# Attention beside projections: small matmuls of one step grouped by array shape, local probabilities turned two slots sooner

## The reference

```python
def stick_breaking_attention(q, k, v):      # 8 heads of 64
    for blk in range(S // BLOCK):           # blocks of 128 queries, keys 0 to the block's end
        z = jnp.einsum('bqhd,bshd->bhqs', qb, kb).astype(jnp.float32) * scale
        strict = s_idx < t_idx
        log_keep = jnp.where(strict, -jax.nn.softplus(z), 0.0)
        tail = lax.cumsum(log_keep, axis=3, reverse=True) - log_keep
        w = jnp.where(strict, jnp.exp(jax.nn.log_sigmoid(z) + tail), 0.0)
        outs.append(jnp.einsum('bhqs,bshd->bqhd', w.astype(v.dtype), vb))

def sliding_window_sink_attention(q, k, v, sinks):   # 8 query heads, 2 key heads, window 128
    scores = jnp.einsum('bnqkgd,bnskd->bnkgqs', qb, k_band).astype(jnp.float32) * scale
    scores = jnp.where(valid[None, :, None, None], scores, -jnp.inf)
    probs = jax.nn.softmax(jnp.concatenate([scores, sink], axis=-1), axis=-1)[..., :-1]
    out = jnp.einsum('bnkgqs,bnskd->bnqkgd', probs.astype(v.dtype), v_band)
```

## Time and profile before

| | |
|---|---|
| median of 3 runs | 2659.11 us (2658.48 to 2659.41) |
| the profiled execution | 2658.53 us |
| its span, first to last instruction | 2657.0 us |
| mean granted clock of TensorE | 0.999 |
| projections, L466 to L468 | 10248 matmuls recorded of 512 columns, 390 to 402 ns each, overlapping |
| first and second attention stage | about 1279 to 1465 us, 1981 to 2168 us |

### The profile page before, as it was taken

How to read it: one execution, slowest core, us unless ns; L and a number is a source line. 1 busy time by engine, 2 the same in 40 slices (tenths; PEclk the granted TensorE clock), 3 DMA queues, 4 the chain that set the end, 5 groups by cost and what they waited for, 6 DMA issues and landing times.

```text
span 2657.0 us, 32191 instructions
## 1 busy us (share of the span) xinstructions
PE 2625.0 (99%) x13046; PEld 2106.6 (79%) x13054; DVE 1514.9 (57%) x2100; ACT 1143.0 (43%) x1694; POOL 161.2 (6%) x147
## 2 busy tenths in 40 slices
PE   8999999999999999999999999999999999999998
PEld 6777778888887888888767888888877778888887
DVE  4566657474778665667765554433456754544433
ACT  6444344242467433335566334322346652423322
POOL 2222010000010000000111000000001100000000
PEclk9999999999999999999999999999999999999999
DMA  4111113222333323322211322223321123223332
GB/s 170 60 60 60 53 55 111 96 95 96 111 95 95 107 95 99 100 96 95 72 59 61 96 95 94 97 95 99 99 80 56 56 80 95 95 95 96 101 97 72
DMA packets 66674, 235.38 MB, mean 89 GB/s; under 512 B 7520, under 2 KB 8160, under 8 KB 66528
## 3 DMA queue, kind: packets, MB, share of 16 engines
q1 hardware_dynamic: 63504, 228.35, 26.7%
q10 hardware_dynamic: 3024, 4.99, 0.6%
HBM read 231.21 MB, written 2.10 MB: 88 GB/s over the span
## 4 chain that ended last, share of the span: by engine, by line
PE 89%; DVE 6%; ACT 3%; issue 2%; DMA 0%; POOL 0%; SPq 0%; ACTq 0%; DVEq 0%
PE bank L466 27%; PE bank L468 27%; PE bank L467 27%; DVE w_lo_k L1490 1%; PE bank L815 1%; PE bank L836 1%; ACT w_hi_k L985 1%; PE bank L885 1%; PE bank L825 1%; DVE xr_lru L1801 0%; PE bank L903 0%; PE bank L893 0%; DVE kept_att L1920 0%; PE bank L676 0%; DVE rot_att L1948 0%
## 5 line engine op out<-in xcount | busy, mean ns | idle before, releaser
L466 PE MATMUL bank<-x_hi_k,w_hi_k 128*128 128x512 f32 x2152 | 865.7, 402 | 12.1 <-DVE x_lo_k L1497 11.2
L468 PE MATMUL bank<-x_hi_k,w_lo_k 128*128 128x512 f32 x2152 | 840.6, 391 | 0.0
L985 ACT ACTIVATE w_hi_k<-raw_k 128x1024 fp32r<-128x1024 f32 x431 | 454.7, 1059 | 895.2 <-PE bank L468 893.6
L467 PE MATMUL bank<-x_lo_k,w_hi_k 128*128 128x512 f32 x2152 | 839.5, 390 | 0.0
L1490 DVE TENSOR_TENSOR w_lo_k<-raw_k,w_hi_k 128x1024 fp32r<-128x1024 f32 x431 | 534.7, 1241 | 166.2 <-ACT w_hi_k L985 165.7
L466 PEld LDWEIGHTS bank<-x_hi_k,w_hi_k 128*128 128x128 f32 x2152 | 404.7, 188 | 110.7 <-issue 14.6
L468 PEld LDWEIGHTS bank<-x_hi_k,w_lo_k 128*128 128x128 f32 x2152 | 404.6, 188 | 86.4
L467 PEld LDWEIGHTS bank<-x_lo_k,w_hi_k 128*128 128x128 f32 x2152 | 405.2, 188 | 82.1 <-issue 4.1
L466 PE MATMUL bank<-y_hi_k,w_hi_k 128*128 128x512 f32 x1136 | 445.6, 392 | 3.2 <-DVE y_lo_k L1836 1.9
L468 PE MATMUL bank<-y_hi_k,w_lo_k 128*128 128x512 f32 x1136 | 442.9, 390 | 0.0
L467 PE MATMUL bank<-y_lo_k,w_hi_k 128*128 128x512 f32 x1136 | 442.8, 390 | 0.0
(11 more groups left out here) (319 smaller groups left out, 2277.1 us busy)
## 6 DMA issues: line engine op xcount, KB each, us to landing
raw_k<-wstream SPq DMA_DIRECT2D x431, 512.0 KB, 3.5
outT<-h_k ACTq DMA_DIRECT2D x8, 256.0 KB, 2.8
h_k<-xT SPq DMA_DIRECT2D x4, 256.0 KB, 8.7
h_k<-xT ACTq DMA_DIRECT2D x4, 256.0 KB, 8.1
decay_mix<-constants ACTq DMA_DIRECT2D x4, 256.0 KB, 2.7
vec_k<-vectors SPq DMA_DIRECT2D x1, 282.5 KB, 10.3
cos_mix<-constants SPq DMA_DIRECT2D x1, 256.0 KB, 10.0
sin_mix<-constants SPq DMA_DIRECT2D x1, 256.0 KB, 10.2
```

The lines of the kernel that those rows point to most:

```text
L466: pe.matmul(dst, wh, rh, start=start, stop=False)
L467: pe.matmul(dst, wh, rl, start=False, stop=False)
L468: return pe.matmul(dst, wl, rh, start=False, stop=stop)
L985: act.activation(k.w_hi[:, u % SPLIT, :], k.raw[:, u % RAW, :], ACT.Copy).then_inc(*hi_done.mark())
```

## The change

TensorE's two lists become one, `pairs_in_step`. All of a step's logits, local scores, outputs and local outputs now stand together in slot 4 of the step, in this order: local masks, logit masks, logits, local scores, output of the step before, local output. So masks are written first (`start=True`) and the products are added to them. The stick's output moves from slot 0 of step g + 2 to slot 4 of step g + 1. The local turning moves from +6 to +4 (`TURN_AT`), the local output from +9 to +6 (`OUT_AT`), and VectorE's low half from +10 to +7; ScalarE's copies move with them. In part 0 the unused block isn't turned nor copied. ScalarE and VectorE keep their two lists.

```diff
+TURN_AT, OUT_AT = 4, 6
...
+        def local_masks(m, part):
             if part == 0:
                 pe.wait_ge(*dve_done.at("wq", layer, m))
...
+        def logit_masks(g):
+            if g % TC == 0:
+                pe.wait_ge(*dve_done.at("qk", layer, g // TC))
+            if g > 0:
+                pe.wait_ge(*act_done.at("stick_wT", layer, g - 1, 1))
+            i = row_tile(g)
+            for half in range(2):
+                pe.matmul(ch(z_view(k, half, i), i), k.id_b[:], k.mask_b[:, 0:P], start=True, stop=False, skip_group_check=True)
+
+        def logits(g):
+            i = row_tile(g)
+            for half in range(2):
+                r = head_rows(half)
+                pe.matmul(z_view(k, half, i), k.aq[r, i * P:i * P + P], k.ak[r, 0:seen_keys(i)], start=False, stop=True,
+                          skip_group_check=True).then_inc(*mark("z", layer, g, half))
...
-        def turned(m, part):
+        def local_turned(m, part):
             pe.wait_ge(*dve_done.at("probs", layer, m, part))
             for half in range(2):
-                for j in range(4):
+                for j in range(1 - part, 4):
                     mm = pe.transpose(ch(bank[6 + half], j), ch(k.p_t[:, half], j), k.ident)
...
+        for slot in range(WINDOW_SLOTS):
+            g, at = divmod(slot, STEP)
+            local = [(m, slot - PAIR_SLOTS * m) for m in range(PAIRS)]
+            scored = [(m, part) for m, t in local for part in range(2) if t == PART_AT[part]]
+            ended = [(m, part) for m, t in local for part in range(2) if t == PART_AT[part] + OUT_AT]
+            if at == 1 and 1 <= g <= ROWS:
+                turned(g - 1, 0)
+            if at == 2 and 1 <= g <= ROWS:
+                turned(g - 1, 1)
+            if at == 3 and g % TC == 0 and g < ROWS:
+                values(g // TC)
+            for m, t in local:
+                if t == norm_slot(m, SUMS_AT):
+                    local_sums(m)
                 for part in range(2):
...
+                    if t == PART_AT[part] + TURN_AT:
+                        local_turned(m, part)
+            if at == 4 and g <= ROWS:
+                for m, part in scored:
+                    local_masks(m, part)
+                if g < ROWS:
+                    logit_masks(g)
+                    logits(g)
+                for m, part in scored:
+                    local_scores(m, part)
+                if g > 0:
+                    output(g - 1)
+                for m, part in ended:
+                    local_output(m, part)
             yield
...
-        interleave(*layer_tasks(stick(layer), window(layer), (Fill(beside_pairs(layer), fill_piece), 0)))
+        steps = (pairs_in_step(layer), WINDOW_SLOTS, 0, 1)
+        interleave(steps, *beside_steps((Fill(beside_pairs(layer), fill_piece), 0)))
...
-                    if at == PART_AT[part] + 6:
+                    if at == PART_AT[part] + TURN_AT:
                         act.wait_ge(*pe_done.at("pT", layer, m, part))
                         for half in range(2):
-                            act.activation(k.pT[:, half, :], bank[6 + half][:], ACT.Copy).then_inc(*mark("pT", layer, m, part))
-                    if at == PART_AT[part] + 9:
+                            act.activation(k.pT[:, half, (1 - part) * P:], bank[6 + half][:, (1 - part) * P:],
+                                           ACT.Copy).then_inc(*mark("pT", layer, m, part))
+                    if at == PART_AT[part] + OUT_AT:
                         act.wait_ge(*pe_done.at("wo", layer, m, part))
...
-                    if at == PART_AT[part] + 10:
+                    if at == PART_AT[part] + OUT_AT + 1:
                         dve.wait_ge(*act_done.at("part_y", layer, m, part))
```

More of the change, by code:

```diff
@@ L368, with beside_steps @@
 SPLIT_LAG, EVICT_LAG, LOW_LAG = 1, 1, 4
-def layer_tasks(stick, window, *fills):
-    tasks = [(stick, STICK_SLOTS, 0, STICK_SLOTS / WINDOW_SLOTS), (window, WINDOW_SLOTS, 0, 1)]
+def beside_steps(*fills):
+    tasks = []
     for fill, lag in fills:
@@ L376, in layer_tasks @@
     return tasks
+def layer_tasks(stick, window, *fills):
+    tasks = [(stick, STICK_SLOTS, 0, STICK_SLOTS / WINDOW_SLOTS), (window, WINDOW_SLOTS, 0, 1)]
+    return tasks + beside_steps(*fills)
 def window_slots():
@@ L796, in final_sums, with pairs_in_step @@
         pe.matmul(bank[6][:], k.ones, k.ssum2[:], start=True, stop=True).then_inc(*mark("norm", "final"))
-    def stick(layer):
+    def pairs_in_step(layer):
         def values(pair):
@@ L805, in values @@
             mm.then_inc(*mark("v_t", layer, pair))
-        def logits(g):
-            i = row_tile(g)
+        def local_masks(m, part):
+            if part == 0:
+                pe.wait_ge(*dve_done.at("wq", layer, m))
+            if part == 1 or m > 0:
+                pe.wait_ge(*dve_done.at("part_y", layer, m - 1 + part, 1 - part))
+            if part == 1 and m + 1 < PAIRS:
+                pe.wait_ge(*act_done.at("wq_mean", layer, m + 1))
+            if part == 0 and m == 0:
+                pe.wait_ge(*act_done.at("wq_mean", layer, 0))
+            masks = k.mask_b[:, 3 * P:5 * P].rearrange("p (o s) -> p o s", o=1).to_broadcast([P, 2, 2 * P])
+            for half in range(2):
+                pe.matmul(bank[6 + half][:], k.id_b[:], masks if part else k.mask_b[:, P:5 * P], start=True, stop=False,
+                          skip_group_check=True)
+        def logit_masks(g):
             if g % TC == 0:
@@ L812, in logits, with local_scores @@
                 pe.wait_ge(*act_done.at("stick_wT", layer, g - 1, 1))
+            i = row_tile(g)
[3 more added lines that the diff above has]
+            i = row_tile(g)
             for half in range(2):
                 r = head_rows(half)
[L815 to L818, removed]
+                pe.matmul(z_view(k, half, i), k.aq[r, i * P:i * P + P], k.ak[r, 0:seen_keys(i)], start=False, stop=True,
+                          skip_group_check=True).then_inc(*mark("z", layer, g, half))
+        def local_scores(m, part):
+            for n in (2 * part, 2 * part + 1):
+                before = max(n - 1, 0) * P
+                to = (n % 2 + 1) * 2 * P
+                for half in range(2):
+                    r = head_rows(half)
+                    mm = pe.matmul(bank[6 + half][:, to - (n + 1) * P + before:to], k.wq[r, n * P:n * P + P], k.wk_t[r, before:(n + 1) * P],
+                                   start=False, stop=n % 2 == 1, skip_group_check=True)
+            mm.then_inc(*mark("scores", layer, m, part))
         def turned(g, half):
@@ L838, in output, with local_sums @@
             mm.then_inc(*mark("att_o", layer, g))
[L840 to L859, removed]
+        def local_sums(m):
             pe.wait_ge(*act_done.at("wq_sq", layer, m))
@@ L865, in sums, with local_output @@
             mm.then_inc(*mark("wq_sum", layer, m))
[L867 to L887, removed]
-        def turned(m, part):
+        def local_turned(m, part):
             pe.wait_ge(*dve_done.at("probs", layer, m, part))
             for half in range(2):
-                for j in range(4):
+                for j in range(1 - part, 4):
                     mm = pe.transpose(ch(bank[6 + half], j), ch(k.p_t[:, half], j), k.ident)
             mm.then_inc(*mark("pT", layer, m, part))
-        def output(m, part):
+        def local_output(m, part):
             n = 2 * part
```

10 lines of the change are left out of this document (removed).

## The result

| | before | changed |
|---|---|---|
| median | 2658.80 us | 2674.01 us |
| profiled execution | 2658.53 us | 2674.08 us |
| its span | 2657.0 us | 2672.6 us |
| mean granted clock | 0.999 | 0.997 |

The changed kernel is slower: ratio 1.0057, 95% interval 1.0042 to 1.0073, 15.2 us by the medians. One of its four executions took 3257.36 us at a mean granted clock of 0.753 and stands outside the comparison. The forecast was 2665.5 us with a range up to 2672.5; the direction was right, the size was not, and the time lies outside the range.

The account below looks back on a forecast made before the run. The prediction took TensorE's work to bound the kernel. From 2658.5 us it took 15.4 for grouping, added 14.7, 6.8 and 2.1 of waits and took 1.2 for waits covered: 2665.5 us, range 2653.5 to 2672.5.

Parts of the forecast that it names:

- Bound: Whole kernel: TensorE, busy 2625.0 of 2657.0 us, sets the end; costs that aren't waits show in distances between starts.
- The price of a change of shape: TensorE's small matmuls in both attention stages: 96 shape changes become 49; gain 15.4 us with the left-out transposes.
- The straight change: TensorE going from 64*128 directly to 128*64, 15 per layer: taken as 0.15 us each, bounds 0 and 0.41.
- The first queries: Step 1's local masks, now ahead of the logits, wait for the rotated queries: 2.1 us added in both layers.
- The waits for the probabilities: TensorE's earlier local turning waits for VectorE's scaled local probabilities: 7.35 us per layer, 14.7 in both.
- The stick's second half: TensorE's turning of stick weights waits longer for GpSimd's product in steps 4, 8, 12: 6.8 us in both layers.
- the sum: Whole kernel's time: 2658.5 - 15.4 + 14.7 + 6.8 + 2.1 - 1.2 = 2665.5 us.
- the first (waits cover each other): Attention stages: gain comes whole, new waits cover one another, 4.2 us per layer left; 2652.4 us; chance 0.16.
- the second (second halves come sooner): Attention stages: probability waits as worked out, stick's second halves cost nothing more; 2658.7 us, no change; chance 0.34.
- The third: Shape changes: less gain (4.2 us less, or 7.8 by dearer straight changes), same waits; 2669.7 to 2673.3 us; chance 0.10.

Follow-up runs that it names:

- e2: The kernel before with only the local turning and ScalarE's copy at +4 for +6, nothing grouped: 2672.62 us, ratio 1.0052.
- e3: The changed kernel with the local turning one slot later, at +5 for +4: 2661.31 us, ratio 1.0006.
- e5: The changed kernel with VectorE's four scalings of local exponentials cut to two of eight columns, output not the reference's: 2661.99 us.
- e6: The changed kernel with VectorE's local low half back at +10 for +7, behind the second scan: 2675.32 us.
- e4: The changed kernel with short bf16 matmuls, results not used, put in front of TensorE's longer waits: 2669.89 us.
- e8: The changed kernel with local turning and output at old slots, query wait behind the logits, stick's outputs at slot 0 of step g + 2: 2654.83 us.

## Why the prediction was wrong in size

- **Bound.** TensorE bounds the kernel, and a cost that isn't a wait shows in the distances of starts: right. Without those distances the change would look like pure loss.
- **The price of a change of shape**: right. The straight change costs 0.15 as taken from the nearest rows, step 4's run 2.62 us for 2.59, step 3 saves 0.49 for 0.49. In all the grouping gave 16.5 us by the distances for 15.4. The 1.1 us more are the 0.5 a layer that the prediction took off where an output is followed directly by transposes: such an output costs only 0.05 less (in the kernel before, an output of step 6 with one transpose behind it takes 0.85 us, alone 0.79, the transpose 0.11).
- **The first queries**: right, 3.7 us of waits for the 1.7 before; 2.1 us were predicted.
- **The waits for the probabilities**: right in mechanism and in size: 13.0 us listed for 14.7, and about 15 by the distances of starts, by which the prediction was worked out; 12 waits in the six parts named. e2, e3 and e5 show the cause from three sides.
- **The stick's second half**: right in mechanism, undersized: 11.7 us listed for 1.2 + 6.8. Steps 4, 8 and 12 wait 2.19, 1.45 and 1.06 us in the first layer, 4.7 for 4.0 predicted; the other 1.1 us per layer are waits in steps 1, 9 and 13, which the prediction doesn't have. Each is followed closely by a wait for the probabilities. Of the low half's 0.42 us ahead of the second scan only 0.20 reach it in step 4; the whole is worth about 0.6 us a layer (e6). What makes the second halves late beyond the predicted sizes no experiment takes apart.
- **The step that failed is the sum**, at two of its terms. It took TensorE's speed as given: the half clock behind the waits isn't in it, nor among the rivals, though it costs 5.1 us by the rows, 4.8 by the stages and 4.1 by the times of e4. And the waits were too small, 27.0 us for 22.4 (24.6 listed), nearly all of it in the waits for GpSimd's product. Of the 8.5 us between forecast and result the clock is 5.1 and the waits 4.6; the larger gain takes 1.1 back. The trace of before could have warned only weakly, since its attention stages hold no idle time over 0.84 us and no fall of the clock.
- **The rivals**: the first (waits cover each other) and the second (second halves come sooner) didn't come true; the waits were larger than in both. The third named less gain at the same waits; the gain was larger than forecast. The 11.2 us that it has if only the late start is saved don't come true (16.5). The upper end of the range was set by it and was 1.5 us too low.

## What to carry to other kernels

Price grouping by shape from the distances of starts around one small run, and then look at what the moved work stood in front of: short work of another chain can be the only thing that hides a latency. Move an order for one reason at a time: the grouping alone made the kernel 3.8 us faster, and 7.4 with the wait moved behind the logits, while turning two slots sooner alone cost 13.4. Where new waits of 1 to 2 us appear on TensorE, the half clock may come behind them (1.7 us each time here); put it into the range. Measure waits by the distances of starts as well: the list of idle times showed 24.6 us of 27.0.

## What the runs showed of the hardware

- Waits of 2.2 us, or of 0.61 and 1.64 us close together, were followed by 3.4 us at a granted clock of 0.5 in the changed kernel; the same pair in its first layer and the same wait of 2.2 us in e5 weren't. Putting 72 short matmuls whose results nobody uses ahead of the waits kept the clock up and made the kernel 4.1 us faster.
- Coming out of a 64\*128 shape cost TensorE 0.10 us where transposes followed (e8, step 6), and out of 128\*64 with its load 0.21 where projections did (step 4 of the changed kernel); going straight from 64\*128 to 128\*64 cost 0.15.
- A VectorE instruction over 1024 columns took 2.00 us beside a GpSimd product and 1.23 behind it; work put between them can be nearly free.
